# A two-layer mixer block on one core: the delta rule's gate rows built by other products, and a projection split around them

## The chip, the cores and the metric

The kernel runs on one core of a Trainium2 chip. The metric is the device time of one execution in microseconds (us); lower is better. Five engines work side by side, each on its own queue of instructions: TensorE (PE, matrix products, with PEld for its weight loads), VectorE (DVE), ScalarE (ACT), GpSimd (POOL) and SyncE (SP, which here issues the loads). They meet only by semaphores.

## The reference

A block of two equal layers works on 512 tokens of width 1024 in float32. Each layer normalises its input, projects it to four mixers (a gated delta rule, a dilated window attention, a stick-breaking attention and a retention), gates and adds their outputs, projects again, and ends with a feed-forward part. The change lies in the delta rule, of which this is the part that matters:

```python
beta = jax.nn.sigmoid(gdn_b.astype(f32)).transpose(0, 2, 1)
g = (-jnp.exp(a_log) * jax.nn.softplus(gdn_a + dt_bias)).transpose(0, 2, 1)
...
gc = jnp.cumsum(g.reshape(B, H, N, C), axis=-1)
decay = jnp.exp(jnp.where(incl, gc[..., :, None] - gc[..., None, :], -jnp.inf))
k_beta = k * beta[..., None]
lower = jnp.where(strict, jnp.einsum('bhncd,bhnsd->bhncs', k_beta, k) * decay, 0.0)
t_inv = triangular_solve(eye + lower, eye)
u = t_inv @ v_beta
w = t_inv @ (k_beta * jnp.exp(gc)[..., None])
...
state = state * jnp.exp(gl) + k_c.T @ v_new
```

There are four heads of width 128. The kernel takes chunks of 128 tokens, four of them, b = 0 to 3.

## The kernel before, in words

**Big products.** Every weight matrix streams in units of 256 rows. SP loads a unit into a stage, POOL splits it into a high and a low float32r part (L568 and L570), and `unit` (L1654, the products on L1686) multiplies: three products (high by high, low by high, high by low) for each of two row blocks and four column tiles, 24 products of 512 columns. The ring has four slots, and POOL may refill one when the first product of the next unit has run (`w_used`).

**PSUM.** Four banks `big0` to `big3` take projections. Four banks `mix0` to `mix3` take everything else. A list, `mixer_keys` (L274), names every use of a `mix` bank in order, and `number` (L215) deals them out in turn: use i of a layer goes to bank i mod 4, and must wait until the use before it in that bank is free. Before, a layer has 316 uses. The list starts again at `mix0` in the second layer, where `PER_LAYER` (L327) says how many uses of each bank the first had. The last four uses are the second feed-forward product of tokens 256 to 511 (`dn0` and `dn1` for t = 2 and 3; `dn0` is columns 0 to 511, `dn1` the rest), and the first uses of the next layer are the transposes of its normalised input for t = 2 and 3 (`turned`, L1734, key `pre1`).

**The delta rule.** Jobs `aq`, `ak`, `aab` and `av` project queries, keys, gate inputs and values. Between the units of `av` stand small jobs (`value_unit`, L1801): sums of squares after units 0 and 1, and after unit 2 the cumulative sum of the gates (key `gc`, L1810) and `decays(0)`. For chunk b and each head, `decays(b)` (L1826) makes in one bank the row of cumulative gates spread over all partitions (`R`: a gate column, broadcast, times the triangle of ones) and in another the row of betas (`B`: a beta column, broadcast, times the identity). These are eight float32 products of 128 columns, which the trace shows as 16 records.

ACT takes the exponential of `R` (L760). DVE waits for it, subtracts (L1301, L1302), clips (L1305) and multiplies the keys by `B` (L1310): `exponents`, L1297. Then ACT does its part (`pair_decays`, L762) and copies the four value tiles (`conv_raw`, L702, keys `raw` 8 to 11), and DVE convolves them (L1262 and L1264, four times three instructions). Behind those DVE has the chain of chunk 0: `lower` (L1316, L1318), `row_decays` (L1339, L1341, L1342), `first_level` (L1325, L1327), `scores_out` (L1332, L1334), and `exponents(1)`. PE runs a unit of a gate projection (`fill`), `lower(0)` and the scores, `decays(1)`, another unit, `lower(1)` and the scores (which need `exponents(1)`), another unit, and then the inversion levels. In the loop over chunks, `decays(2)` and `decays(3)` stand right before a `fill`.

**Waits that matter later.** `lower(b)` on PE waits for L1310 of the chunk. In the order of bank uses `R`, `B` of chunk 1 follow four places behind `raw` 10 and `raw` 11, so they wait until DVE has convolved those. A bank of the second feed-forward product is freed by `residual` (L1122, instruction L1127).

Of the kernel before, what the change touches and what calls it, by code (L numbers as in the profile page):

```python
# [17 lines left out]
F32R = mybir.dt.float32r  # L18
# [5 lines left out]
P = 128  # L24
# [41 lines left out]
def stick_at(e, j):  # L66
# [8 lines left out]

CI, CTU, CLV, CMG0, CMG1, CMG2, CSEL, CRD, CRR, CNTL, CNTU, CNEG, CEND = np.cumsum(
    [0, P, P, 7 * P, 512, P, P, 2 * DH, P, P, P, P, 8]).tolist()
ROT = CEND - CRD
# [7 lines left out]
def shape_constants():  # L86
# [16 lines left out]
    def rotation(half):  # L103
        r = np.zeros((P, P), np.float32)
        for b in range(0, P, DH):
            for i in range(half):
                r[b + i + half, b + i] = -1.0
                r[b + i, b + i + half] = 1.0
        return r
# [3 lines left out]
         neg(np.concatenate([first, near], 1)), neg(c <= p),  # L113
         neg((c <= p) & ((p - c) % 4 == 0)), sel, rotation(8), rotation(32), -one(c <= p), -one(c > p), -one(c + p >= 0)[:, 0:8]], 1)
    return np.ascontiguousarray(consts.astype(np.float32))
# [158 lines left out]
def mixer_keys():  # L274
# [3 lines left out]
    k += [("l2", i) for i in range(4)] + ["ab"] + [("l2", i) for i in range(4, 8)]  # L278
    k += ["gc", ("R", 0), ("B", 0)] + [("raw", i) for i in range(8, 12)]
    k += [("LT", 0), ("att", 0), ("R", 1), ("B", 1), ("LT", 1), ("att", 1)]  # L280
# [48 lines left out]
    "a_g": 2, "a_kbe": 4, "a_ln": 8, "a_lt": 4, "a_lt0": 4, "a_ltc": 4, "a_min": 4, "a_nrm": 4, "a_ohi": 4,  # L329
    "a_olo": 4, "a_out": 4, "a_qd": 4, "a_rs": 8, "a_sc": 3, "a_silu": 12, "a_small": 2, "a_smallact": 4, "a_sq": 8,  # L330
    "a_tap": 24, "a_z": 4, "an_rs": 4, "an_sq": 4, "b_exp": 36, "b_fc": 3, "b_fexp": 3, "b_max": 12, "b_nm": 12,
    "b_ohi": 5, "b_olo": 5, "b_rhi": 9, "b_rlo": 9, "b_rp": 9, "b_share": 2, "b_sum": 3, "b_zinv": 1, "b_zln": 1,
    "big_done0": 43, "big_done1": 43, "big_done2": 38, "big_done3": 38, "big_free0": 43, "big_free1": 43,
    "big_free2": 38, "big_free3": 38, "c_act": 40, "c_add": 8, "c_bias": 3, "c_exp": 20, "c_half": 4, "c_hi": 8,
    "c_ln": 20, "c_ohi": 4, "c_pos": 20, "c_pv": 4, "c_pvfree": 4, "c_split": 8, "c_sum": 20, "c_z": 20, "d_nrm": 4,
    "d_ohi": 4, "d_olo": 4, "d_out": 4, "d_rope": 4, "d_rp": 4, "dn_rs": 4, "dn_sq": 4, "f_hi": 32, "f_lo": 32,
    "f_relu": 32, "gated_b": 8, "gated_c": 8, "gated_d": 8, "m_hi": 8, "mix_done0": 79, "mix_done1": 79,
# [10 lines left out]
def hybrid_kernel(nc, ins, out):  # L348
    ctx = ExitStack()
    with ctx:  # L350
# [743 lines left out]
        def vector_layer(dve, l):  # L1094
# [133 lines left out]
            if l == 0:  # L1228
# [420 lines left out]
        def tensor_layer(pe, l):  # L1649
# [151 lines left out]
            def value_unit(i):  # L1801
                if i == 0:
                    l2_sums(0, 1, 2, 3)
                if i == 1:
                    gates_by_token()
                    l2_sums(4, 5, 6, 7)
                if i == 2:
                    pe.wait_ge(*upto("a_g", 2))
                    ps = tile_of("gc")
                    done(MM(ps[:, 0:16], triu, s_g.rearrange("p b h -> p (b h)"), start=True, stop=True), "gc")  # L1810
                    decays(0)

# [13 lines left out]
            def decays(b):  # L1826

                per_head_tile(("R", b), lambda o_, h: MM1(o_, s_g[:, b, h:h + 1].to_broadcast((P, P)), triu))
                per_head_tile(("B", b), lambda o_, h: MM1(o_, s_be[:, b, h:h + 1].to_broadcast((P, P)), ident))

# [12 lines left out]
            do("aab")  # L1843
            do("av", between=value_unit)
            set_fill("gatea0", "az")
# [474 lines left out]
```

## Time and profile before

| | |
|---|---|
| median of 3 runs | 2381.67 us (2379.85 to 2381.67) |
| the profiled execution | 2382.03 us, its span 2380.2 us |
| PE busy | 2340.7 us, 98% of the span |
| POOL / DVE / ACT busy | 1283.1 / 890.0 / 771.4 us |
| mean granted clock of PE | 0.996 |

The span is the part that the profiler covers. PE is the engine that hardly ever rests, and the chain that ended last is 91% PE. A record's length is longer than the distance to the next record, because products overlap: the distance between starts is what a product costs on a full PE. The two layers look alike: what stands at 92.51 us in the first stands at 1272.91 us in the second, 1180.4 us later, and so it goes for the rows around.

### The profile page before, as it was taken

Reading aid. Unit: us, or ns where it says so; the run is one execution under the profiler, and the core shown is the slowest. Engines: PE = TensorE matmul, PEld = TensorE weight load, DVE = VectorE, ACT = ScalarE, POOL = GpSimd, SP = SyncE. Lnnn points to the kernel's source line nnn. Section 1 sums busy time; section 2 is a strip of 40 time slices with the busy share of each in tenths; the row PEclk is TensorE's granted clock in tenths of the full one; section 3 lists DMA queues with packets and bytes.
Section 4 is the critical chain, followed back from the end, with each engine's and each line's share of the span. In section 5 each row is a group of like instructions: output and inputs, shape, how many; then the busy total and the mean of one; then the engine's idle time right before and its main releaser. Section 6 shows DMA issues by size and latency. Waiting matters only on the chain.

```text
span 2380.2 us, 29590 instructions
## 1 busy us (share of the span) xinstructions
PE 2340.7 (98%) x11798; PEld 1917.6 (81%) x11798; DVE 890.0 (37%) x1404; ACT 771.4 (32%) x1537; POOL 1283.1 (54%) x732
## 2 busy tenths in 40 slices
PE   8999999999999999999999999999999999999998
PEld 7798877787877888888887988767778778888887
DVE  3653314343355431123356523243443445211233
ACT  5533325323136231122355442262140353211121
POOL 5511653564553566677655126635555535666774
PEclk9999999999999999999999999999999999999999
DMA  4300331332231333333223013313322313333331
GB/s 152 98 27 28 89 89 53 98 89 72 79 100 44 106 107 97 98 98 98 80 77 89 19 36 91 87 47 113 89 80 71 93 49 95 119 98 97 97 95 66
DMA packets 105753, 196.84 MB, mean 83 GB/s; under 512 B 8464, under 2 KB 18832, under 8 KB 105360
## 3 DMA queue, kind: packets, MB, share of 16 engines
q1 hardware_dynamic: 104464, 188.65, 26.2%
q10 hardware_dynamic: 1152, 6.29, 0.8%
q8 instruction: 95, 1.56, 0.3%
q14 instruction: 42, 0.34, 0.0%
HBM read 192.82 MB, written 2.10 MB: 82 GB/s over the span
## 4 chain that ended last, share of the span: by engine, by line
PE 91%; DVE 5%; ACT 3%; issue 1%; DMA 0%; DVEq 0%; ACTq 0%
PE big L1686 66%; PE mix L1686 9%; PE mix L1824 5%; DVE c_lo L1429 1%; PE big L2000 1%; PE mix L1968 1%; PE mix L1894 1%; PE mix L2069 1%; PE mix L1979 1%; PE mix L1787 1%; PE mix L2201 1%; PE mix L2150 0%; DVE scr L1441 0%; PE mix L1741 0%; PE mix L2134 0%
## 5 line engine op out<-in xcount | busy, mean ns | idle before, releaser
L568 POOL TENSOR_SCALAR ring_hi<-stage 128x1024 fp32r<-128x1024 f32 (+3 forms) x364 | 372.1, 1022 | 1042.6 <-PE big L1686 962.2
L570 POOL TENSOR_TENSOR ring_lo<-stage,ring_hi 128x1024 fp32r<-128x1024 f32 (+3 forms) x364 | 912.6, 2507 | 30.4
L1686 PE MATMUL big<-h_hi,ring_hi 128*128 128x512 f32 (+1 forms) x1888 | 720.3, 382 | 2.8 <-DVE h_lo L1149 1.5
L1686 PE MATMUL big<-h_hi,ring_lo 128*128 128x512 f32 (+1 forms) x1888 | 709.9, 376 | 0.0
L1686 PE MATMUL big<-h_lo,ring_hi 128*128 128x512 f32 (+1 forms) x1888 | 709.9, 376 | 0.0
L1686 PEld LDWEIGHTS big<-h_hi,ring_hi 128*128 128x128 f32 x1888 | 355.7, 188 | 75.3 <-issue 9.0
L1686 PEld LDWEIGHTS big<-h_lo,ring_hi 128*128 128x128 f32 x1888 | 355.6, 188 | 65.4
L1686 PEld LDWEIGHTS big<-h_hi,ring_lo 128*128 128x128 f32 x1888 | 355.8, 188 | 63.8 <-issue 1.9
L1628 DVE TENSOR_TENSOR h_lo<-scr,h_hi 128x1024 fp32r<-128x1024 f32 x64 | 84.7, 1324 | 248.4 <-ACT h_hi L1067 248.4
L1686 PE MATMUL big<-ring_hi,h_hi 128*128 128x512 f32 x448 | 174.5, 391 | 0.0
L1686 PE MATMUL big<-ring_lo,h_hi 128*128 128x512 f32 x448 | 174.3, 391 | 0.0
L1686 PE MATMUL big<-ring_hi,h_lo 128*128 128x512 f32 x448 | 173.9, 390 | 0.0
L1067 ACT ACTIVATE h_hi<-scr 128x1024 fp32r<-128x1024 f32 x64 | 67.9, 1061 | 262.7 <-PE big L1686 260.7
L1639 DVE SCALAR_TENSOR_TENSOR scr<-big,scr 128x512 f32<-128x512 f32 x64 | 44.2, 691 | 254.5 <-ACT scr L1076 254.4
L1824 PE MATMUL mix<-scr 128*128 128x128 f32 (+1 forms) x1088 | 131.0, 276 | 1.3 <-DVE scr L1397 0.7
L1824 PEld LDWEIGHTS mix<-scr 128*128 128x128 f32 x1088 | 126.2, 192 | 4.6 <-DVE scr L1397 1.2
L1686 PE MATMUL mix<-ring_hi,h_hi 128*128 128x512 f32 x320 | 125.2, 391 | 0.0
L1686 PE MATMUL mix<-ring_hi,h_lo 128*128 128x512 f32 x320 | 124.7, 390 | 0.0
L1686 PE MATMUL mix<-ring_lo,h_hi 128*128 128x512 f32 x320 | 124.7, 390 | 0.0
L1076 ACT ACTIVATE scr<-big 128x512 f32<-128x512 f32 x64 | 38.3, 599 | 262.1 <-PE big L1686 261.2
L1686 PEld LDWEIGHTS big<-ring_hi,h_hi 128*128 128x128 f32 x448 | 84.1, 188 | 18.2 <-issue 0.7
L1686 PEld LDWEIGHTS big<-ring_hi,h_lo 128*128 128x128 f32 x448 | 84.2, 188 | 17.6
(292 smaller groups left out, 2826.3 us busy)
## 6 DMA issues: line engine op xcount, KB each, us to landing
stage<-in_w_in SPq DMA_DIRECT2D x168, 512.0 KB, 3.5
stage<-in_w_mlp_in SPq DMA_DIRECT2D x64, 512.0 KB, 3.6
stage<-in_w_mlp_out SPq DMA_DIRECT2D x64, 512.0 KB, 3.8
stage<-in_w_o SPq DMA_DIRECT2D x16, 512.0 KB, 3.8
stage<-in_w_br_a SPq DMA_DIRECT2D x8, 512.0 KB, 3.8
stage<-in_w_br_c SPq DMA_DIRECT2D x8, 512.0 KB, 3.8
stage<-in_w_br_d SPq DMA_DIRECT2D x8, 512.0 KB, 3.9
stage<-in_w_br_b SPq DMA_DIRECT2D x8, 512.0 KB, 3.5
```

Of the source, the lines that this page charges most:

```text
L568: nc.gpsimd.tensor_scalar(rH[jw][0:pp, r, 0:kk, 0:job.n], w, 1.0, 0.0, ALU.mult, ALU.add).then_inc(sem("w_hi"), 1)
L570: nc.gpsimd.tensor_tensor(rL[jw][0:pp, r, 0:kk, 0:job.n], w, f32(rH[jw][0:pp, r, 0:kk, 0:job.n]), ALU.subtract).then_inc(sem("w_ready"), 1)
L1067: A(hH[:, q:q + 2, :], fT[:, 2 * u:2 * u + 2, :], ACT.Copy).then_inc(sem("f_hi"), 1)
L1076: A(fT[:, 4 * g + i, :], ps[:, :], ACT.Relu).then_inc(sem("f_relu"), 1)
L1429: TT(c_L[:, us, :], c_S[:, us, :], f32(c_H[:, us, :]), ALU.subtract).then_inc(sem("c_split"), 1)
L1628: TT(hL[:, q:q + 2, :], fT[:, 2 * u:2 * u + 2, :], f32(hH[:, q:q + 2, :]), ALU.subtract).then_inc(sem("f_lo"), 1)
L1639: big_free(STT(fT[:, k, :], ps[:, :], 0.0, fT[:, k, :], ALU.max, ALU.mult), (f"up{g}", i))
L1686: ins_ = MM(o_, a_, r_, start=s0, stop=s1)
L1787: done(MM(ps[:, :], f32(ones_r[:, 0:1]).to_broadcast((P, P)), q_sq[:, i % 4, :], start=True, stop=True), ("l2", i))
L1824: return MM(o_, a_, b_, start=True, stop=True)
L1894: i = TR(ps[:, q * P:(q + 1) * P], g_T(e, h), ident)
L1968: i = MM(c_bank[u][:, at:at + w], hv(cK, h)[:, j * P:(j + 1) * P], hv(cQ, h)[:, j * P:], start=opens, stop=True, skip_group_check=True)
```

## The change

The gates and betas are no longer spread one head at a time. The cumulative gates and betas of all chunks (32 columns, `s_begc`) are transposed by two float32 products into a new `mix` use, key `gt`, in which even heads lie on partitions 0 to 15 and odd heads on 32 to 47. DVE splits them into a high float32r part and, 64 partitions further down, a low part, in a tile `g_rows` of 256 columns that was zeroed at the layer's start. `decays(b)` then is four float32r products of 256 columns (two for `R`, two for `B`): a new 16-column selector, broadcast, picks the four partitions of one row of the tile. `gc` moves one unit earlier, behind the sums of squares after unit 1. `decays(0)` moves from in front of `av`'s last unit into its middle, behind the column tiles 0 and 1. The list of bank uses becomes 317 long.

```diff
-    k += ["gc", ("R", 0), ("B", 0)] + [("raw", i) for i in range(8, 12)]
+    k += ["gc", "gt", ("R", 0), ("B", 0)] + [("raw", i) for i in range(8, 12)]
...
-    ... "mix_done0": 79, ... "mix_free0": 79, ...
+    ... "mix_done0": 80, ... "mix_free0": 80, ...
...
+        s_begc = st[:, 80:112].rearrange("p (r e) -> p e r", e=2)
...
+            V.memset(f32(g_rows[:, :]), 0.0).then_inc(sem("a_zero"), 1)
             V.memset(g_S, 0.0).then_inc(sem("a_S0"), 1)
...
+            ps = mix_wait(dve, "gt")
+            dve.wait_ge(*upto("a_zero", 1))
+            for e in range(2):
+                rows, cols = slice(32 * e, 32 * e + 16), slice(e * P, (e + 1) * P)
+                TS(g_rows[rows, cols], ps[rows, cols], 1.0, None, ALU.mult).then_inc(sem("a_rhi"), 1)
+            for e in range(2):
+                rows, low, cols = slice(32 * e, 32 * e + 16), slice(64 + 32 * e, 80 + 32 * e), slice(e * P, (e + 1) * P)
+                dve.wait_ge(*upto("a_rhi", e + 1))
+                i = TT(g_rows[low, cols], ps[rows, cols], f32(g_rows[rows, cols]), ALU.subtract)
+            mix_free(i, "gt")
...
                 if i == 1:
                     gates_by_token()
                     l2_sums(4, 5, 6, 7)
-                if i == 2:
                     pe.wait_ge(*upto("a_g", 2))
                     ps = tile_of("gc")
                     done(MM(ps[:, 0:16], triu, s_g.rearrange("p b h -> p (b h)"), start=True, stop=True), "gc")
-                    decays(0)
+                if i == 2:
+                    mix_freed(pe, "gc")
+                    ps = tile_of("gt")
+                    MM1(ps[0:16, 0:P], s_begc[:, 0, :], ident)
+                    done(MM1(ps[32:48, P:2 * P], s_begc[:, 1, :], ident), "gt")
...
             def decays(b):
 
-                per_head_tile(("R", b), lambda o_, h: MM1(o_, s_g[:, b, h:h + 1].to_broadcast((P, P)), triu))
-                per_head_tile(("B", b), lambda o_, h: MM1(o_, s_be[:, b, h:h + 1].to_broadcast((P, P)), ident))
+                mix_freed(pe, "gt")
+                for name, row in (("R", 8), ("B", 0)):
+                    ps = tile_of((name, b))
+                    for q in range(2):
+                        at = CROW - CRD + row + 2 * b + q
+                        i = MM1(ps[:, 2 * P * q:2 * P * (q + 1)], rot_r[:, at:at + 1].to_broadcast((P, P)), g_rows[:, :])
+                    done(i, (name, b))
...
-            do("av", between=value_unit)
+            for i in range(3):
+                unit(JOB["av"], i)
+                value_unit(i)
+            unit(JOB["av"], 3, (0, 1))
+            decays(0)
+            unit(JOB["av"], 3, (2, 3))
```

In the changed program every line number is higher: L1686 becomes L1699, L1741 becomes L1754, L1810 becomes L1822, L1824 becomes L1840.

First place, on PE, between the units 2 and 3 of `av` in the first layer, before:

```order
L1686 MATMUL big0<-h_lo,ring_hi 128x512
L1810 MATMUL mix1<-st,consts 128x16 [waits mix_free1,a_g]
L1824 MATMUL mix2<-consts,st 128x128 [waits mix_free2]
L1824 MATMUL mix2<-consts,st 128x128 x3
L1824 MATMUL mix3<-consts,st 128x128 [waits mix_free3]
L1824 MATMUL mix3<-consts,st 128x128 x3
L1686 MATMUL big1<-h_hi,ring_hi 128x512 [waits w_ready]
```

and now, where the rows left out are the rest of unit 3's first half (`big1` and `big2`):

```order
L1699 MATMUL big0<-h_lo,ring_hi 128x512
L1840 MATMUL mix2<-consts,st 16x128 [waits mix_free2,mix_free1]
L1840 MATMUL mix2<-consts,st 16x128
L1699 MATMUL big1<-h_hi,ring_hi 128x512 [waits w_ready]
...
L1699 MATMUL big2<-h_lo,ring_hi 128x512
L1840 MATMUL mix3<-g_rows_51,rot_r 128x256 [waits mix_free3,mix_free2]
L1840 MATMUL mix3<-g_rows_51,rot_r 128x256
L1840 MATMUL mix0<-g_rows_51,rot_r 128x256 [waits mix_free0]
L1840 MATMUL mix0<-g_rows_51,rot_r 128x256
L1699 MATMUL big3<-h_hi,ring_hi 128x512 [waits w_ready]
```

The first `R` (here in `mix3`) now comes behind twelve more products of 512 columns, and L1810 has left for the place one unit earlier.

Second place, on PE, after the first gate unit behind `av`: `lower(0)`, the scores and `decays(1)`, now:

```order
L1840 MATMUL mix1<-scr 128x128 [waits mix_free0,mix_free3,mix_free1,mix_free2]
L1840 MATMUL mix1<-scr 128x128 x3
L1840 MATMUL mix2<-scr 128x128 [waits mix_free2]
L1840 MATMUL mix2<-scr 128x128 x3
L1840 MATMUL mix3<-g_rows_51,rot_r 128x256 [waits mix_free3,mix_free2]
L1840 MATMUL mix3<-g_rows_51,rot_r 128x256
L1840 MATMUL mix0<-g_rows_51,rot_r 128x256 [waits mix_free0]
L1840 MATMUL mix0<-g_rows_51,rot_r 128x256
L1699 MATMUL big1<-h_hi,ring_hi 128x512 [waits w_ready]
```

Its order is that of before; the waits on `mix3` and `mix0` are for the convolutions of `raw` 10 and 11, as they were (then in `mix2` and `mix3`).

Third place, on PE, at the start of the second layer: the last product of `dn1` for t = 3 and the transposes for t = 2, before:

```order
L1686 MATMUL mix3<-ring_hi,h_hi 128x512 [waits w_ready]
...
L1686 MATMUL big1<-h_lo,ring_hi 128x256
L1741 MATMUL mix0<-consts,scr 128x128 [waits pre1_h,mix_free0]
L1741 MATMUL mix0<-consts,scr 128x128 x3
L1741 MATMUL mix1<-consts,scr 128x128 [waits pre1_h,mix_free1]
L1741 MATMUL mix1<-consts,scr 128x128 x3
L1686 MATMUL big2<-h_hi,ring_hi 128x256 [waits big_free2,w_ready]
```

and now:

```order
L1699 MATMUL mix0<-ring_hi,h_hi 128x512 [waits w_ready]
...
L1699 MATMUL big1<-h_lo,ring_hi 128x256
L1754 MATMUL mix0<-consts,scr 128x128 [waits pre1_h,mix_free0]
L1754 MATMUL mix0<-consts,scr 128x128 x3
L1754 MATMUL mix1<-consts,scr 128x128 [waits pre1_h,mix_free1]
L1754 MATMUL mix1<-consts,scr 128x128 x3
L1699 MATMUL big2<-h_hi,ring_hi 128x256 [waits big_free2,w_ready]
```

The transposes stand where they stood and go to the same bank, `mix0`; the bank's use before them is now `dn1` for t = 3, where it was `dn0` for t = 2.

## Rows read from the trace of the kernel before

**Rows 1.** The page: span and the chain that ended last, by engine.

```profile
span 2380.2 us, 29590 instructions
PE 91%; DVE 5%; ACT 3%; issue 1%; DMA 0%; DVEq 0%; ACTq 0%
```

**Rows 2.** Timeline of PE around `decays(0)`: start, length, engine, line, operation.

```profile
92.38 0.29 PE L1810 MATMUL mix<-st,consts 128*128 128x16 f32 x2
92.51 2.03 PE L1824 MATMUL mix<-consts,st 128*128 128x128 f32 x16
94.30 0.48 PE L1686 MATMUL big<-h_hi,ring_hi 128*128 128x512 f32 x1
94.61 0.40 PE L1686 MATMUL big<-h_hi,ring_lo 128*128 128x512 f32 x1
```

**Rows 3.** Timeline of PE, products of 256 columns in job `aq`.

```profile
26.61 0.28 PE L1686 MATMUL big<-h_hi,ring_lo 128*128 128x256 f32 x1
26.73 0.28 PE L1686 MATMUL big<-h_lo,ring_hi 128*128 128x256 f32 x1
```

**Rows 4.** Timeline of ACT, behind `decays(0)`.

```profile
93.69 0.60 ACT L760 ACTIVATE scr<-mix 128x512 f32<-128x512 f32 x1 [4.65 <-PE mix L1824]
96.30 0.63 ACT L764 ACTIVATE scr<-scr 128x512 f32<-128x512 f32 x1 [2.01 <-DVE scr L1305]
```

**Rows 5.** Timeline of DVE from `exponents(0)` to the chain of chunk 1.

```profile
95.21 1.05 DVE L1305 TENSOR_SCALAR scr<-scr 128x512 f32<-128x512 f32 x1
...
98.15 1.53 DVE L1262 SCALAR_TENSOR_TENSOR scr<-mix,lw,scr 128x511 f32<-128x511 f32 x2 [1.29 <-ACT scr L709]
...
106.39 0.75 DVE L1264 SCALAR_TENSOR_TENSOR scr<-mix,lw,scr 128x509 f32<-128x509 f32 x1
...
108.39 0.16 DVE L1339 COPY st<-scr 128x4 f32<-128x4 f32 x1
...
109.74 0.70 DVE L1325 TENSOR_TENSOR mix<-mix,consts 128x512 f32<-128x512 f32 x1
...
113.20 0.43 DVE L1305 TENSOR_SCALAR scr<-scr 128x512 f32<-128x512 f32 x1
...
116.81 0.98 DVE L1339 COPY st<-scr 128x4 f32<-128x4 f32 x1
...
118.31 2.88 DVE L1342 TENSOR_TENSOR scr<-scr 128x512 f32<-128x512 f32 x1
121.11 0.69 DVE L1325 TENSOR_TENSOR mix<-mix,consts 128x512 f32<-128x512 f32 x1
```

**Rows 6.** Timeline of POOL in the same stretch.

```profile
94.94 1.05 POOL L568 TENSOR_SCALAR ring_hi<-stage 128x1024 fp32r<-128x1024 f32 x1 [3.96 <-PE big L1686]
...
116.72 1.05 POOL L568 TENSOR_SCALAR ring_hi<-stage 128x1024 fp32r<-128x1024 f32 x1 [3.58 <-PE big L1686]
117.86 2.77 POOL L570 TENSOR_TENSOR ring_lo<-stage,ring_hi 128x1024 fp32r<-128x1024 f32 x1
```

**Rows 7.** Timeline of PE: `decays(1)`, the unit behind it, `lower(1)`.

```profile
107.10 1.95 PE L1824 MATMUL mix<-consts,st 128*128 128x128 f32 x16
108.81 0.47 PE L1686 MATMUL big<-h_hi,ring_hi 128*128 128x512 f32 x1
...
114.36 1.97 PE L1824 MATMUL mix<-scr 128*128 128x128 f32 x16
```

**Rows 8.** Timeline of PE, the unit behind `decays(3)`.

```profile
168.41 0.48 PE L1686 MATMUL big<-h_hi,ring_hi 128*128 128x512 f32 x1
```

**Rows 9.** Timeline of DVE beside it.

```profile
167.85 0.16 DVE L1339 COPY st<-scr 128x4 f32<-128x4 f32 x1
```

**Rows 10.** Timeline of PE, transposes for t = 2 of the second layer.

```profile
1197.54 1.24 PE L1741 MATMUL mix<-consts,scr 128*128 128x128 f32 x8
```

**Rows 11.** Timeline of DVE, the two residuals of t = 3.

```profile
1200.10 1.41 DVE L1127 SCALAR_TENSOR_TENSOR x_sb<-mix,st,x_sb 128x512 f32<-128x512 f32 x2
```

**Rows 12.** Busy time by stretch: PE, PEld, DVE, ACT, POOL, PE clock, DMA, GB/s.

```profile
16.00:19.00 3.00, 2.89 (x13) 2.92 (x14) 1.46 (x8) 2.16 (x8) 2.94 (x2) 0.50 1.06 389
```

More of the change, by code:

```diff
@@ L73 @@
 RING = 4
-CI, CTU, CLV, CMG0, CMG1, CMG2, CSEL, CRD, CRR, CNTL, CNTU, CNEG, CEND = np.cumsum(
-    [0, P, P, 7 * P, 512, P, P, 2 * DH, P, P, P, P, 8]).tolist()
+CI, CTU, CLV, CMG0, CMG1, CMG2, CSEL, CRD, CRR, CNTL, CNTU, CNEG, CROW, CEND = np.cumsum(
+    [0, P, P, 7 * P, 512, P, P, 2 * DH, P, P, P, P, 8, 16]).tolist()
 ROT = CEND - CRD
@@ L113, in shape_constants @@
          neg(np.concatenate([first, near], 1)), neg(c <= p),
-         neg((c <= p) & ((p - c) % 4 == 0)), sel, rotation(8), rotation(32), -one(c <= p), -one(c > p), -one(c + p >= 0)[:, 0:8]], 1)
+         neg((c <= p) & ((p - c) % 4 == 0)), sel, rotation(8), rotation(32), -one(c <= p), -one(c > p), -one(c + p >= 0)[:, 0:8], one(p % 32 == c)[:, 0:16]], 1)
     return np.ascontiguousarray(consts.astype(np.float32))
@@ L329 @@
     "a_g": 2, "a_kbe": 4, "a_ln": 8, "a_lt": 4, "a_lt0": 4, "a_ltc": 4, "a_min": 4, "a_nrm": 4, "a_ohi": 4,
[L330 to L337, printed above, removed]
[1 row of a table removed]
+    "a_olo": 4, "a_out": 4, "a_qd": 4, "a_rhi": 2, "a_rs": 8, "a_sc": 3, "a_silu": 12, "a_small": 2, "a_smallact": 4,
+    "a_sq": 8, "a_tap": 24, "a_z": 4, "a_zero": 1, "an_rs": 4, "an_sq": 4, "b_exp": 36, "b_fc": 3, "b_fexp": 3,
+    "b_max": 12, "b_nm": 12, "b_ohi": 5, "b_olo": 5, "b_rhi": 9, "b_rlo": 9, "b_rp": 9, "b_share": 2, "b_sum": 3,
+    "b_zinv": 1, "b_zln": 1, "big_done0": 43, "big_done1": 43, "big_done2": 38, "big_done3": 38, "big_free0": 43,
+    "big_free1": 43, "big_free2": 38, "big_free3": 38, "c_act": 40, "c_add": 8, "c_bias": 3, "c_exp": 20, "c_half": 4,
+    "c_hi": 8, "c_ln": 20, "c_ohi": 4, "c_pos": 20, "c_pv": 4, "c_pvfree": 4, "c_split": 8, "c_sum": 20, "c_z": 20,
+    "d_nrm": 4, "d_ohi": 4, "d_olo": 4, "d_out": 4, "d_rope": 4, "d_rp": 4, "dn_rs": 4, "dn_sq": 4, "f_hi": 32,
+    "f_lo": 32, "f_relu": 32, "gated_b": 8, "gated_c": 8, "gated_d": 8, "m_hi": 8, "mix_done0": 80, "mix_done1": 79,
[1 row of a table added]
     "mixed_b": 8, "n2_half": 4, "n2_ln": 4, "n2_nw": 8, "n2_ss": 8, "n2_v": 4, "n2_w": 8, "n2_y": 4, "n4_half": 4,
@@ L367, in hybrid_kernel @@
         idb, strictb = (nc.alloc_sbuf_tensor_at(n, [P, P], BF16, offset=scr_at + 4 * at) for n, at in (("idb", 19456), ("strictb", 19520)))
+        g_rows = nc.alloc_sbuf_tensor_at("g_rows", [P, 2 * P], F32R, offset=scr_at + 4 * 19712)
         c_hi = nc.alloc_sbuf_tensor_at("c_hi", [P, 5 * S], F32R, offset=scr_at + 4 * C_HIGH)
```

2 rows, old and new, of the table PER_LAYER are left out of this document.

## The prediction, made before the changed kernel was run

> **What bounds the kernel now.** I read the page first: a span of 2380.2 us whose last chain is 91% PE [rows 1]. So each us taken from PE is worth a us, unless something else is late in its place. The change is local, so I then went through the timelines of PE, DVE, ACT and POOL from 90 to 185 us, and looked for the moments in which PE stands against another engine. There are two kinds. DVE works without a break from its first value convolution at 98.15 to the end of `exponents(1)`; PE's `lower(1)` at 114.36 starts just when that is done [rows 5, 7]. And at the start of layer 2 the transposes for t = 2 begin at 1197.54, while DVE's last residual ends at 1200.10 + 1.41 = 1201.51 [rows 10, 11]. Nothing waits for that residual there now. Both layers show the same rows 1180.4 us apart, so all below but the layer border counts twice.
>
> **The products themselves.** Sixteen records of `decays(1)` take 108.81 - 107.10 = 1.71 us, 0.107 each; `decays(0)` takes 94.30 - 92.51 = 1.79 [rows 2, 7]. A float32r product of 256 columns costs 26.73 - 26.61 = 0.12 [rows 3], with another stationary matrix each time, so four cost 0.48. Going from float32 to float32r lengthens one gap (0.31 between 94.30 and 94.61, where 0.23 is usual), once before and once after. `decays` of chunks 1 to 3 thus lose 1.23 each, `decays(0)` 1.31. The two transposes of `gt` are four records more, 0.43. `gc` only moves; it takes 0.13 either way. If nothing else were late, a layer would win 3 x 1.23 + 1.31 - 0.43 = 4.57, the kernel 9.1.
>
> **Layer part, step 1: `R` of chunk 0 comes later.** `gt` ends at 92.51 + 0.43 = 92.94. Twelve products of unit 3 at 0.227 (24 of them and a switch took 114.36 - 108.81 = 5.55, [rows 7]) and one switch of 0.08 bring PE to 95.74. The second `R` product starts at 95.86. Before, ACT began L760 at 93.69, 0.40 after the last `R` record had started (92.51 + 7 x 0.11) [rows 2, 4]; so now 96.26, which is 2.57 later. DVE's clipping L1305 started at 95.21 and took 1.05 because POOL's L568 ran from 94.94; alone it takes 0.43 [rows 5, 6]. Now it starts at 97.78, POOL has finished both its instructions by then, and it ends at 98.21 where it was 96.26: ACT's L764 starts 1.95 later than at 96.30 [rows 4]. The value copies and convolutions follow in the same queues: DVE starts them at 100.10 instead of 98.15 and ends them at 109.09 instead of 107.14 [rows 5].
>
> DVE's four new instructions (two copies of 16 rows, two subtractions) have to fit between 93.2 and 95.74. The nearest rows are a small copy at 0.16 alone and at 0.98 when POOL is in the way [rows 5]. Four times 0.16 is hidden; four times 0.98 would cost 1.4 more. I take nothing: the value is nearer to the free copy, since a copy out of PSUM is not the kind that the rows show stretched, and even one stretched instruction is hidden. The memset at the layer's start is hidden too (0.16 to 1.05, with all of `aq`, `ak` and most of `av` between it and its reader). The earlier `gc` needs gates that DVE has had since before; no wait is added.
>
> **Step 2: PE waits at `decays(1)`.** PE ends `av` at 95.74 + 0.48 + 2.72 = 98.94, the gate unit at 104.38, `lower(0)` and scores (16 records like `decays` and a switch, 1.78) at 106.16. `R` waits for the third convolution, `B` for the fourth: 109.14. The next unit starts at 109.4, where it was 108.81 [rows 7]. So all that PE won so far is gone, and 0.6 us more. Behind the waiting `B` stand the unit and `lower(1)`.
>
> **Step 3: the unit's start sends POOL into DVE's chain.** POOL's L568 starts 0.64 after the first product of a unit (94.94 - 94.30) [rows 2, 6]: at 110.04. DVE's L1339 comes 1.25 after the last convolution (108.39 - 107.14), at 110.34. That is the meeting that chunk 1 already shows: L568 at 116.72, L1339 at 116.81 stretched to 0.98, L570 at 117.86, and L1342 stretched to 2.88 (L1325, of the same size, takes 0.69), so that L1325 starts at 121.11, 4.39 after L568 [rows 5, 6]. In chunk 0 it was missed, and L1325 started at 109.74. Now it starts at 110.04 + 4.39 = 114.43, which is 4.69 later. Only 1.95 of it is step 1; 2.74 is the collision. `exponents(1)` ends 4.69 later, and PE, which is ready at 109.4 + 5.44 = 114.84, starts `lower(1)` at 114.36 + 4.69 = 119.05. From there to the inversion all engines keep the distances they had. Step 3 lies between 0 (no meeting) and 2.74; by the row nearest in kind, chunk 1's, I take 2.74.
>
> The Trainium skill ("SBUF — State Buffer", section "Who interferes with whom") says that a DVE instruction with two SBUF inputs, or in its two-port mode, and a GpSimd instruction never share their ports: the second one blocks. The trace agrees, with the 2.88. By that rule the collision is all or nothing, so a middle value would be wrong.
>
> **Step 4: `decays(2)`** keeps its 1.23: PE's next needs of DVE there are several us old, and what follows waits for PE's own `lower(2)`.
>
> **Step 5: `decays(3)`.** Its unit starts at 168.41 [rows 8], and relative to DVE it would start 1.23 earlier, at 167.18; POOL follows at 167.82, DVE's L1339 stands at 167.85 [rows 9]. So here too the unit would come just early enough to put L568 and L570 in front of L1342, which ACT's L760 waits for. Between 1.23 kept and 0.1 lost; I take 0.3 kept, since the rows have POOL first, if only by 0.03.
>
> Per layer: + 4.69 - 1.23 - 0.3 = + 3.2, so + 6.4 for two.
>
> **The border of the layers.** 317 uses are one more than four times 79. The transposes for t = 2 now wait for `dn1` of t = 3, which is freed at 1201.51, and start at 1201.56 instead of 1197.54: + 4.0, once. Nothing hides it: PE is in order, and behind it stand the whole of `aq`'s first half. What ACT and DVE do for t = 3 slides along by 2.5 to 4 us and stays ahead of PE. There is no deadlock, since the residual needs nothing of these transposes. The bound below is 0, if that bank were free sooner than the row says; above, the 4.0.
>
> **Sum.** 6.4 + 4.0 = 10.4 us on top of the profiled 2382.03 us. Counted from the median of 2381.67, which is 0.4 lower and what the time will be compared with, that is **2392.1 us**.
>
> **The rivals.**
> *The clock falls in the new pauses.* After the sparse start PE ran at the lower level: from 16 to 19 us the granted clock was 0.50 (1.2 GHz), after PE had waited for its first inputs [rows 12]. That stretch cost half of 2.89, 1.4 us. The new pauses of about 4 us (twice before `lower(1)`, once at the border) have no like in the trace of before. For it speaks their length, against it that PE is full on both sides. One to three times 1.4: 2393.5 to 2396.3. The Trainium skill ("TensorE: Matmul & The Clock Gate", section "HAM oscillation") says that idle gaps put the array back to half rate. By it this rival is real; no row here shows it behind a full PE.
>
> *No collision.* If POOL misses DVE in both places, a layer changes by 1.95 - 1.23 - 1.23 = - 0.5, two by - 1.0, and the border remains: 2384.7. For it speaks that 0.3 us decides in step 3; against it that both sides hang on the same event, the last convolution.
>
> *The border costs nothing*, steps 1 to 5 as told: 2381.67 + 6.4 = 2388.1. For it speaks only that the bank numbers are read from a list and not from a row.
>
> *The other side: faster.* If `decays(0)` in the middle of unit 3 delays nobody, because ACT and DVE catch up in the 1.29 us that DVE idles before 98.15 and behind it, PE keeps its 9.1 us. With the border that is 2381.67 - 9.1 + 4.0 = 2376.6, without it 2372.6. It decides in its favour if `lower(1)` starts before about 112.2. Against it: those 1.29 us are ACT's own chain behind L1305, which moves as a whole, and from there DVE has no gap.
>
> **How the numbers follow.** Chances: the forecast 0.48, the falling clock 0.18, the border for nothing 0.10, no collision 0.13, faster 0.11. From no change this measurement can tell about 0.2%, 4.8 us. Forecast, clock and free border lie above 2386.4: slower 0.76. No collision is + 3.0: same 0.13. Faster 0.11. The range goes from the no-collision case, 2384.3, to the clock's upper end, 2396.5, and leaves out the faster case and a little above.
>
> **What would show it.** Right: PE's first `R` product at about 95.7; the first value convolution near 100.1; a pause of PE of about 2 us before `B` of chunk 1 and of about 4 us before `lower(1)`, with L1342 of chunk 0 stretched to over 2 us; the transposes of layer 2 about 4 us behind the last half-width product before them; PE's busy time less by 7 to 10 us although the span is longer. Wrong: no stretched L1342 in chunk 0 (step 3), the convolutions less than 1 us later (step 1), a `decays` that takes over 1 us (the products), or a granted clock of 0.5 anywhere after 20 us (the first rival).

## The result, and the profile after

The changed kernel takes 2393.96 us (median of 5 runs, 2393.00 to 2394.73), the kernel before 2381.67 (5 runs, 2379.85 to 2382.12): a ratio of 1.0056, 95% interval 1.0046 to 1.0067. It is slower by 12.3 us by the medians (13.3 by the ratio); 2392.1 was forecast.

The page of the changed kernel, against [rows 1], with the waits of PE summed over the execution (line waited at, releaser, us in total, times, longest):

```profile
span 2392.2 us, 29436 instructions
PE 2336.6 (98%) x11710; PEld 1911.8 (80%) x11710; DVE 896.1 (37%) x1414; ACT 771.8 (32%) x1537; POOL 1284.8 (54%) x732
PE 88%; DVE 6%; ACT 3%; issue 2%; DMA 0%; DVEq 0%; ACTq 0%
```

```profile
PE mix L1840 <- DVE scr L1323: 9.4, 4, 3.8
...
PE mix L1754 <- DVE x_sb L1129: 4.1, 1, 4.1
...
PE mix L1840 <- DVE scr L1267: 2.4, 2, 1.2
...
PE big L1699 <- ACT scr L711: 1.9, 2, 1.0
```

PE has less to do (2336.6 us against 2340.7), the span is 12 us longer, and the last chain has 3% less of PE. The four waits are new, and each names a place: L1840 is `decays` and `lower`, L1754 the transposes at the layer border, L1699 a weight unit. Line numbers are 2 to 26 higher than before: L1305 is now L1318, L1310 L1323, L1339 L1352, L1342 L1355, L1325 L1338, L568 L570.

PE in the first layer, answering to [rows 2, 7]: start, length, engine, line, operation, count, and in brackets how long it stood and for whom.

```profile
95.26 0.64 PE L1840 MATMUL mix<-g_rows,rot_r 128*128 128x256 f32 x4
95.74 0.40 PE L1699 MATMUL big<-h_hi,ring_hi 128*128 128x512 f32 x1
...
99.61 0.47 PE L1699 MATMUL big<-h_hi,ring_hi 128*128 128x512 f32 x1 [0.95 <-ACT scr L711]
...
106.89 0.48 PE L1840 MATMUL mix<-g_rows,rot_r 128*128 128x256 f32 x2
108.55 0.50 PE L1840 MATMUL mix<-g_rows,rot_r 128*128 128x256 f32 x2 [1.18 <-DVE scr L1267]
```

```profile
118.34 2.66 PE L1840 MATMUL mix<-scr 128*128 128x128 f32 x16 [3.83 <-DVE scr L1323]
```

The four products of `decays(0)` take 95.74 - 95.26 = 0.48 us where sixteen took 1.79. And then PE stands: 1.18 before `B` of chunk 1, 3.83 before `lower(1)`. What it stands for is in DVE's timeline, answering to [rows 5], and POOL's, answering to [rows 6]:

```profile
99.50 1.53 DVE L1265 SCALAR_TENSOR_TENSOR scr<-mix,lw,scr 128x511 f32<-128x511 f32 x2 [1.28 <-ACT scr L711]
...
109.74 0.78 DVE L1352 COPY st<-scr 128x4 f32<-128x4 f32 x1
110.42 0.68 DVE L1354 TENSOR_TENSOR scr<-scr 128x512 f32<-128x512 f32 x1
111.03 2.88 DVE L1355 TENSOR_TENSOR scr<-scr 128x512 f32<-128x512 f32 x1
113.83 0.68 DVE L1338 TENSOR_TENSOR mix<-mix,consts 128x512 f32<-128x512 f32 x1
...
121.79 1.53 DVE L1355 TENSOR_TENSOR scr<-scr 128x512 f32<-128x512 f32 x1
```

```profile
109.44 1.05 POOL L570 TENSOR_SCALAR ring_hi<-stage 128x1024 fp32r<-128x1024 f32 x1 [5.66 <-PE big L1699]
110.58 2.77 POOL L572 TENSOR_TENSOR ring_lo<-stage,ring_hi 128x1024 fp32r<-128x1024 f32 x1
```

The first value convolution starts at 99.50 instead of 98.15, on a trace whose start happened to be 0.6 us shorter (the sums of `l2` start at 82.75 instead of 83.35), so 1.95 later. PE begins the next unit behind `B`, POOL's split of the weights starts 0.55 us after that, and DVE's L1355, which takes 0.68 alone, takes 2.88 beside POOL's L572.

The border, answering to [rows 10, 11], and the granted clock behind the two long pauses (window; length, busy PE, PEld, DVE, ACT, POOL; the third number from the end is the clock):

```profile
1204.73 1.71 PE L1754 MATMUL mix<-consts,scr 128*128 128x128 f32 x8 [4.13 <-DVE x_sb L1129]
```

```profile
114.00:118.00 4.00, 0.51 (x3) 0.09 (x1) 3.90 (x8) 0.86 (x2) 0.00 (x0) 1.00 0.48 133
118.00:119.00 1.00, 0.66 (x5) 0.66 (x6) 0.29 (x1) 0.45 (x2) 0.00 (x0) 1.00 0.00 0
119.00:120.00 1.00, 1.00 (x10) 1.00 (x9) 0.46 (x1) 0.00 (x0) 0.00 (x0) 0.81 0.00 0
120.00:122.00 2.00, 2.00 (x8) 1.80 (x8) 1.82 (x5) 0.60 (x1) 0.40 (x1) 0.50 0.00 0
122.00:123.00 1.00, 1.00 (x4) 0.72 (x3) 1.00 (x1) 0.00 (x0) 0.92 (x2) 0.50 0.00 0
123.00:124.00 1.00, 1.00 (x6) 0.82 (x5) 0.96 (x3) 0.00 (x0) 1.00 (x1) 0.99 0.00 0
...
1206.00:1208.00 2.00, 2.00 (x12) 2.00 (x11) 1.13 (x4) 2.00 (x8) 1.92 (x2) 0.50 0.59 135
```

PE stands from about 114.5 to 118.3, goes on at the full clock (1.00), and a microsecond later is at 0.50, the lower of its two levels, until about 123. The same follows the wait at the border.

**Where the 12 us are.** The starts of like records in both traces, after minus before: -0.60 at the sums of `l2`, +3.98 at `lower(1)`, +4.69 at the end of chunk 1's inversion (129.08 against 124.39), +3.41 behind `decays(2)`, +3.18 ahead of the border, +8.37 behind it, then +12.74 at `lower(1)` of layer 2 and +11.96 in the end. So the first layer costs 3.8 (3.18 and the 0.60), the second 3.6 and the border 5.2.

### The profile page after: what moved, and what is told of

Same layout as the page of the kernel before. It is cut to its first block, busy times and chain, and to the rows that moved or that the text cites. A ratio compares the mean times of both kernels' runs of the same rounds, so it can differ in the third digit from the quotient of the medians.

```text
span 2392.2 us, 29436 instructions
## 1 busy us (share of the span) xinstructions
PE 2336.6 (98%) x11710; PEld 1911.8 (80%) x11710; DVE 896.1 (37%) x1414; ACT 771.8 (32%) x1537; POOL 1284.8 (54%) x732
## 4 chain that ended last, share of the span: by engine, by line
PE 88%; DVE 6%; ACT 3%; issue 2%; DMA 0%; DVEq 0%; ACTq 0%
PE big L1699 65%; PE mix L1699 9%; PE mix L1840 5%; DVE c_lo L1442 1%; PE big L2026 1%; PE mix L1994 1%; PE mix L1920 1%; PE mix L2095 1%; PE mix L2005 1%; PE mix L1800 1%; DVE scr L1355 1%; DVE scr L1265 1%; PE mix L2227 0%; PE mix L2176 0%; DVE scr L1454 0%
## 5 line engine op out<-in xcount | busy, mean ns | idle before, releaser
L570 POOL TENSOR_SCALAR ring_hi<-stage 128x1024 fp32r<-128x1024 f32 (+3 forms) x364 | 371.4, 1020 | 1052.8 <-PE big L1699 972.2
L572 POOL TENSOR_TENSOR ring_lo<-stage,ring_hi 128x1024 fp32r<-128x1024 f32 (+3 forms) x364 | 914.9, 2514 | 30.4
L1699 PE MATMUL big<-h_hi,ring_hi 128*128 128x512 f32 (+1 forms) x1888 | 720.1, 381 | 4.6 <-ACT scr L711 1.9
L1699 PE MATMUL big<-h_hi,ring_lo 128*128 128x512 f32 (+1 forms) x1888 | 710.5, 376 | 0.0
L1699 PE MATMUL big<-h_lo,ring_hi 128*128 128x512 f32 (+1 forms) x1888 | 710.3, 376 | 0.0
L1699 PEld LDWEIGHTS big<-h_hi,ring_hi 128*128 128x128 f32 x1888 | 356.5, 189 | 77.0 <-issue 11.4
L1699 PEld LDWEIGHTS big<-h_lo,ring_hi 128*128 128x128 f32 x1888 | 356.3, 189 | 65.9
L1699 PEld LDWEIGHTS big<-h_hi,ring_lo 128*128 128x128 f32 x1888 | 356.6, 189 | 63.3 <-issue 1.4
L1699 PE MATMUL big<-ring_lo,h_hi 128*128 128x512 f32 x448 | 174.3, 391 | 0.0
L1699 PE MATMUL big<-ring_hi,h_hi 128*128 128x512 f32 x448 | 174.3, 391 | 0.0
L1699 PE MATMUL big<-ring_hi,h_lo 128*128 128x512 f32 x448 | 173.9, 390 | 0.0
L1840 PE MATMUL mix<-scr 128*128 128x128 f32 (+1 forms) x1088 | 134.1, 280 | 10.8 <-DVE scr L1323 9.4
L1840 PEld LDWEIGHTS mix<-scr 128*128 128x128 f32 x1088 | 128.3, 195 | 15.7 <-DVE scr L1323 10.6
L1699 PE MATMUL mix<-ring_hi,h_hi 128*128 128x512 f32 x320 | 125.1, 391 | 0.0
L1699 PE MATMUL mix<-ring_hi,h_lo 128*128 128x512 f32 x320 | 124.7, 390 | 0.0
L1699 PE MATMUL mix<-ring_lo,h_hi 128*128 128x512 f32 x320 | 124.7, 390 | 0.0
L1699 PEld LDWEIGHTS big<-ring_hi,h_hi 128*128 128x128 f32 x448 | 84.2, 188 | 18.1 <-issue 0.7
L1699 PEld LDWEIGHTS big<-ring_lo,h_hi 128*128 128x128 f32 x448 | 83.8, 188 | 18.2 <-POOL ring_lo L572 1.1
```

Of the source, the lines that this page charges most:

```text
L570: nc.gpsimd.tensor_scalar(rH[jw][0:pp, r, 0:kk, 0:job.n], w, 1.0, 0.0, ALU.mult, ALU.add).then_inc(sem("w_hi"), 1)
L572: nc.gpsimd.tensor_tensor(rL[jw][0:pp, r, 0:kk, 0:job.n], w, f32(rH[jw][0:pp, r, 0:kk, 0:job.n]), ALU.subtract).then_inc(sem("w_ready"), 1)
L1699: ins_ = MM(o_, a_, r_, start=s0, stop=s1)
L1840: return MM(o_, a_, b_, start=True, stop=True)
```

## The experiments

All were timed beside the kernel before, whose medians in the three sessions were 2379.94 (e1 to e4), 2380.26 (e5 to e8) and 2379.93 us (e9 to e11). Ratios are to it. The changed kernel was timed in a session of its own, where the kernel before took 2381.67; so a distance to it is given twice, by the medians and by the ratios. The interval of a ratio is some 2 to 3 us to either side, so smaller differences between experiments rest on the traces. In kernels with the gate (e2) or ACT's order (e6) the line numbers are up to 4 higher again.

**e1: the border alone mended**, by another order of the last four bank uses:

```diff
-    k += [(f"dn{hf}", t) for t in (2, 3) for hf in range(2)]
+    k += [("dn1", 2), ("dn0", 3), ("dn1", 3), ("dn0", 2)]
```

> The changed kernel with the four last bank uses of a layer dealt in another order, so that the first transposes of layer 2 again go to a bank that dn0 of t = 2 used before. Theory (the border of the layers costs a wait and, behind it, a stretch at the lower clock): PE starts those transposes without the 4.1 us wait and keeps the full clock there, 4.1 + 1.1 = 5.2 us less than the changed kernel's 2393.96, so about 2388.8 us, ratio to the kernel before 1.0030. Rival A (the clock falls there anyway): 2389.9. Rival B (the bank is not what the transposes wait for): no change, 2394.

Measured: 2388.40 us, ratio 1.0036 (1.0024 to 1.0049), 5.6 us under the changed kernel by the medians, 4.8 by the ratios. The wait for `x_sb` is gone and the clock is 1.00 from 1190 to 1215; it still falls behind the pause at 118. By the times the border cost 4.8 to 5.6, with some 3 us of interval, and 5.2 in the trace; 4.0 was forecast.

**e4: the border alone put into the kernel before**, by an order that gives the transposes the same late bank:

```diff
-    k += [(f"dn{hf}", t) for t in (2, 3) for hf in range(2)]
+    k += [("dn1", 3), ("dn1", 2), ("dn0", 3), ("dn0", 2)]
```

> The kernel before, with nothing changed but the order of the four last bank uses, so that the first transposes of layer 2 go to the bank that dn1 of t = 3 used. Theory: the border's wait appears here alone, 4.0 us, and with it the lower clock for about 2.2 us of products: 2381.67 + 5.1 = 2386.8 us, ratio 1.0021. Rival A (the clock falls only together with what else the change does): 2385.7. Rival B (another part of the change makes the border wait): 2381.7.

Measured: 2385.66, ratio 1.0026 (1.0016 to 1.0035): 5.7 us slower by the medians and 6.2 by the ratio, with nothing else changed. The theory's difference was 5.1, that of rival A 4.0; the time alone doesn't part the two, but the trace does. The wait is there with the same length, and the clock falls with it:

```profile
PE mix L1741 <- DVE x_sb L1127: 4.1, 1, 4.1
```

```profile
1202.00:1204.00 2.00, 1.72 (x9) 1.72 (x9) 0.23 (x1) 0.57 (x3) 2.00 (x2) 0.50 0.47 176
1204.00:1206.00 2.00, 2.00 (x12) 2.00 (x11) 1.30 (x5) 2.00 (x9) 1.92 (x2) 0.50 0.79 214
```

So the border is 4.1 of wait and some 1 to 2 of clock, from both sides.

**e2: POOL held back.** Its split waits until DVE has done the L1355 of that chunk:

```diff
+                chained = {3: 1, 4: 2, 6: 3}.get(u - UNIT_AT["gatea0", 1])
+                if chained:
+                    pool.wait_ge(*upto("a_kbe", chained))
```

> The changed kernel with GpSimd held back: before it splits the three weight units that fall next to DVE's row_decays (chunks 0, 1 and 3), it waits until DVE has finished them. Theory (POOL's two instructions block DVE's two-input instructions, and that is most of what lower(1) waits for): L1355 of chunk 0 takes 0.69 instead of 2.88 us, lower(1) comes only about 2 us later than before instead of 4.6, the clock doesn't fall behind it, decays(3) keeps its 1.2 us. About 5 us less per layer, 10 in all: 2384 us, ratio to before 1.001. Rival (DVE's chain is late for the later R alone): L1355 is short but lower(1) still comes over 4 us late, and the time stays within 2 us of 2394. Second rival (holding POOL back starves PE of weights): slower than 2394, with PE waiting for POOL's L574.

Measured: 2385.69, ratio 1.0023 (1.0013 to 1.0033), 8.3 us under the changed kernel (7.9 by the ratios); 10 was expected. PE and DVE of e2:

```profile
116.15 2.05 PE L1843 MATMUL mix<-scr 128*128 128x128 f32 x16 [1.26 <-DVE scr L1326]
```

```profile
110.13 0.16 DVE L1355 COPY st<-scr 128x4 f32<-128x4 f32 x1
110.20 0.68 DVE L1357 TENSOR_TENSOR scr<-scr 128x512 f32<-128x512 f32 x1
110.80 0.68 DVE L1358 TENSOR_TENSOR scr<-scr 128x512 f32<-128x512 f32 x1
```

The small copy is back from 0.78 to 0.16 and the 2.88 to 0.68; the pause before `lower(1)` shrinks from 3.83 to 1.26, and the clock is 1.00 from 110 to 125. The inversion of chunk 1 ends 4.2 us earlier counted from the sums of `l2`; twice that is 8.4. No wait of PE for POOL came in its place, so the second rival is out.

**e8: the gate for chunk 0 alone** (`{3: 1}`).

> The changed kernel with POOL held back for chunk 0 alone; chunks 1 and 3 collide as they did. My step 3: this collision costs 2.74 a layer, 2.2 by the row of lower(1), and the pause falls under the length behind which the clock fell, 0.7 more: -5.8 in two layers, 2388.2, ratio 1.0035. Rival: all that the gate won (8.3 us) comes from chunk 0, the others collide for nothing: 2385.7, ratio 1.0023. Other rival: the clock falls behind a pause of 1.3 to 2 us as well: 2389.5.

Measured: 2388.38, ratio 1.0032 (1.0020 to 1.0045), 5.6 under the changed kernel (5.7 by the ratios): the theory's number, 2388.2, though the interval also holds the two rivals. The collision of chunk 0 costs 2.8 us a layer with the clock that fell behind it. The other chunks collide for 1.1 to 1.3 more, by the difference to e2; the times alone would not show that, but the trace does: L1358 of chunk 1 is 2.88 again, and PE stands 0.33 and 0.24 in the inversion and 0.85 in chunk 3, where e2 has 0, 0 and 0.15.

**e3: border and gate.**

> Both edits together. Theory: the two costs are separate in time and add, 2394 - 5.2 - 10 = 2378.8 us, ratio 0.9988. Rival (they share something, such as the clock): less than the sum, over 2381.

Measured: 2379.10, where 2378.8 was expected; ratio 0.9995 (0.9986 to 1.0003). Within the intervals the two costs add up: 4.8 and 7.9 by the ratios make 12.7, and both mends together bring 14.5. Without them the kernel can't be told from the one before, though PE has less to do. What is left is step 1, which neither mend touches: `lower(1)` still comes 2.0 later than before, counted from the sums of `l2` (32.99 against 31.01).

**e10: the place alone.** The kernel before, its float32 `decays` untouched, no `gt`, no change at the border:

```diff
-            do("av", between=value_unit)
...
+            unit(JOB["av"], 3, (0, 1))
+            decays(0)
+            unit(JOB["av"], 3, (2, 3))
```

> The kernel before with its float32 decays as they were, no g_rows and no gt, only the place of the change: decays(0) between the halves of unit 3. The count of bank uses and the border stay as before. Theory: the place is what costs, by DVE's chain: R of chunk 0 is 12 products at 0.227 and a switch, 2.8 us, later, L1305 loses its 0.6 of being stretched, DVE's convolutions start 2.2 later, PE waits at decays(1), and its unit then sends POOL into L1342 of chunk 0, 2.7 more. 4 to 5 us a layer: 2389.5, ratio 1.004. Rival: without the fourfold faster products PE comes to decays(1) later and waits little, so POOL misses L1342: 2 us a layer or less, under 2385. Second rival: place costs nothing (under 2382) and the products' own chain through DVE is to blame.

Measured: 2387.23, ratio 1.0027 (1.0017 to 1.0038): slower by 7.3 by the medians and 6.4 by the ratio, less than the theory's 9.6 and more than the 5.1 that its rival allowed. The interval (4 to 9 us) doesn't quite exclude that rival, and three of the eight runs, the profiled one among them, lie at 2383.9 to 2384.8, the others at 2387.0 to 2388.0. In the trace the end of chunk 1's inversion comes 2.9 later than before, counted from the sums of `l2` (43.91 against 41.04). PE stands 0.53 before `B` of chunk 1 and 1.19 before `lower(1)`. DVE and POOL of e10:

```profile
99.86 1.53 DVE L1262 SCALAR_TENSOR_TENSOR scr<-mix,lw,scr 128x511 f32<-128x511 f32 x2 [1.28 <-ACT scr L709]
...
110.77 1.53 DVE L1342 TENSOR_TENSOR scr<-scr 128x512 f32<-128x512 f32 x1
```

```profile
110.46 1.30 POOL L568 TENSOR_SCALAR ring_hi<-stage 128x1024 fp32r<-128x1024 f32 x1 [6.31 <-PE big L1686]
111.84 2.72 POOL L570 TENSOR_TENSOR ring_lo<-stage,ring_hi 128x1024 fp32r<-128x1024 f32 x1
```

The convolutions are 2.1 later (99.86 - 98.15, and 0.39 of a shorter start), as expected. L1342 met POOL's first instruction instead of its second, so it was stretched to 1.53 and not to 2.88. So the half-way place is a loss in itself, also without new products: some 3 us a layer. The second rival is out.

**e5: `decays(0)` one tile earlier**, on top of e3:

```diff
-            unit(JOB["av"], 3, (0, 1))
+            unit(JOB["av"], 3, (0,))
             decays(0)
-            unit(JOB["av"], 3, (2, 3))
+            unit(JOB["av"], 3, (1, 2, 3))
```

> The changed kernel with the border's banks in the old order, POOL's splits held back behind L1342 of the chunk, and decays(0) one tile earlier in unit 3 (after the first of its four tiles). Theory: the products are worth their 1.23 us each wherever PE is what the end hangs on, and what the change lost was the place of decays(0) and the two collisions of its consequences. One tile of unit 3 is three hi/lo products plus a weight switch less ahead of R, some 1.4 us, so the first convolution starts 0.5 us after the kernel before's instead of 1.95, PE waits at decays(1) for about 0 and a layer wins 1.23 (decays(2)) + 1.23 (decays(3)) + some of decays(1): 2375 us, ratio 0.998 of the kernel before. Rival: ACT's order (L760 behind what has been queued since) decides, not PE, and the tile earlier is worth nothing: 2379, ratio 0.9995, as with the two mends alone.

Measured: 2377.71, ratio 0.9987 (0.9979 to 0.9996). Between theory (2375) and rival (2379). `R` came 1.36 earlier, but DVE's clipping then met POOL again and took 1.01 instead of 0.43, so the convolutions came only some 0.75 earlier.

**e11: `decays(0)` before the whole of unit 3**, on top of e3, straight behind `gt`.

> The changed kernel with border and gate mended, and decays(0) before the whole of unit 3, straight behind gt, as the kernel before had it. PE then stands about 1.3 us for DVE's four instructions that make g_rows (in e5 the first tile of unit 3, 1.36 us, lay over them). Theory: PE waits 1.2 us before decays(1) anyway, so this stand only takes the place of that wait and DVE's chain starts as in e5: the same as e5 within 1 us, 2378.0, ratio 0.999. Rival: PE's stand adds to the end, 1.3 a layer: 2380.3, ratio 1.0000.

Measured: 2376.02, ratio 0.9982 (0.9973 to 0.9991). The theory expected e5 within 1 us; this is 1.7 under it by the medians and 1.2 by the ratios. PE of e11:

```profile
93.94 0.73 PE L1843 MATMUL mix<-g_rows,rot_r 128*128 128x256 f32 x4 [1.37 <-DVE g_rows L1310]
...
107.12 0.72 PE L1843 MATMUL mix<-g_rows,rot_r 128*128 128x256 f32 x4
```

PE stands 1.37 us in the open, and the kernel is not slower for it: the wait inside `decays(1)` is gone in exchange. Filling that gap with half a unit, as the change did (e3), cost 3.1 us more by the ratios, whose intervals just overlap.

**e6: e5, and ACT makes the first raw copy before the pair exponentials of chunk 0:**

```diff
             key_decays(0)
+            conv_raw(8)
             pair_decays(0)
-            for i in range(8, 12):
+            for i in range(9, 12):
                 conv_raw(i)
```

> The same, and ACT makes the first raw copy of av before the exponentials of chunk 0's pair, so that DVE has a convolution to do in the 1.28 us that it stood idle. Theory: DVE's unbroken row from the first value convolution to exponents(1) is what PE's lower(1) hangs on, so an earlier first convolution is worth up to 1 us a layer: 2373 us, ratio 0.997. Rival: ACT's other instructions slide behind by the same 0.6 us and the L764 that DVE's own chunk 0 needs comes late: nothing, 2375.

Measured: 2372.34, where 2373 was expected; ratio 0.9969 (0.9956 to 0.9981). This beats both kernels: by the ratio it is 7.4 us under the one before. PE of e6:

```profile
107.20 0.50 PE L1844 MATMUL mix<-g_rows,rot_r 128*128 128x256 f32 x2 [0.29 <-DVE scr L1271]
114.40 2.05 PE L1844 MATMUL mix<-scr 128*128 128x128 f32 x16 [1.25 <-DVE scr L1327]
```

Counted from the sums of `l2`, `lower(1)` comes 1.4 us earlier than in e5, against the 1 that was expected. The rival's 2375 is still inside the interval, but by it this start would not have moved.

**e9: the same order of ACT in the kernel before**, with the gate for its chunk 1. **e7: that gate alone** (`{4: 2}`).

> The kernel before, with the two mends that do not need the change: ACT makes the first raw copy of av before the pair exponentials of chunk 0, and POOL's split of chunk 1 waits behind L1342. Theory: before the change PE is without a gap up to lower(1), so an earlier DVE has nothing to give; what e6 won, it won because the shorter decays left PE room. 2379.5 us, ratio 0.9997 of the kernel before. Rival: ACT's order is the gain in itself and the products only came with it: ratio 0.998 or less, under 2376.

> The kernel before, with nothing changed but POOL's split of the ring behind L1342 of chunk 1, whose 2.88 us the trace of before shows. Theory of the collision (a blocked DVE instruction costs what it is longer than 0.69, as far as PE waits on it): PE waited 1.4 for L1327 in chunk 1, so 0.6 us a layer: 2378.7 against 2379.9, ratio 0.9995, hardly to be told from none; L1342 then takes about 0.7 in the trace. Rival: POOL's split, 3.8 us later, makes the next unit late: PE waits on the ring, and the time is over 2381.

Measured: e9 2382.02, ratio 1.0003 (0.9995 to 1.0012); e7 2380.01, ratio 1.0001 (0.9992 to 1.0010). ACT's order is worth nothing there: `lower(1)` starts 31.0 us behind the sums of `l2` in e7, in e9 and in the kernel before, as PE is without a gap. So what e6 won needs the shorter `decays`. For e7 1.2 us less was expected, too little to be told from none. Its trace has chunk 1's inversion end 1.0 us earlier in layer 1, and the times don't show the 2 us that this would make in two layers (see the last section).

## Why the prediction was right

*The products* were right: 0.48 us for `decays(0)` and 170.57 - 170.02 = 0.55 for `decays(3)`, where 0.48 was said. PE's busy time fell by only 4.1 us where 7 to 10 was named as a sign; the records at the slower clock are longer, by some 4.5 us in all (an estimate from the trace: 1.7 a layer and 1.1 at the border, see below), and 4.1 + 4.5 = 8.6.

*Step 1* was right to the digit: convolutions 1.95 later. It missed a wait: the first tile of the gate unit needs the bank of the first `av` tile, which ACT frees only after its own delayed chain (0.95 at 99.61). It cost nothing, since PE had to stand before `B` anyway: the pause there was 1.18 and not the 2 that was said, as the other 0.95 had been stood before.

*Step 2* was right. The unit after `decays(1)` starts at 108.89 + 0.60 = 109.49; 109.4 was said.

*Step 3* was right, and e2 and e8 show its cause: `lower(1)` moved by 3.98 + 0.60 = 4.58 where 4.69 was forecast. But the sentence drawn from the page "SBUF — State Buffer" of the Trainium skill (section "Who interferes with whom"), that a middle value would be wrong, is not borne out. How much is lost depends on which of POOL's two instructions it meets: the 0.68 us instruction took 1.53 beside the first (which took 1.19 in chunk 1 of the changed kernel and 1.30 in e10) and 2.88 beside the second, of 2.77 us.

*Step 4* was right: +5.29 at the end of chunk 1's inversion and +4.01 behind `decays(2)`, both with the 0.60 added, so 1.28 was kept where 1.23 was said.

*Step 5*: `decays(3)` kept 0.23, 0.3 was said. The collision in chunk 3 is there as forecast:

```profile
171.25 0.95 DVE L1352 COPY st<-scr 128x4 f32<-128x4 f32 x1
...
172.71 2.88 DVE L1355 TENSOR_TENSOR scr<-scr 128x512 f32<-128x512 f32 x1
```

*The border*: the wait is 4.13, 4.0 was said.

*The range* was given as 2384.3 to 2396.5, where the cases that it names come to 2384.7 and 2396.3; the measured time lies within either.

*What failed* is the rival that was set beside the forecast instead of in it: the clock. It fell behind all three pauses of about 4 us. At the border it cost 1.1 in the trace (5.2 less 4.1). In a layer it cost 1.7. Here are the starts of the inversion of chunk 1 and of what follows it, first before and then now:

```profile
121.62 0.60 PE L1860 MATMUL mix<-consts,scr 128*128 128x128 f32 x4
...
124.39 3.69 PE L1824 MATMUL mix<-scr 128*128 128x128 f32 x32
```

```profile
127.34 1.03 PE L1886 MATMUL mix<-consts,scr 128*128 128x128 f32 x8
...
129.08 3.69 PE L1840 MATMUL mix<-scr 128*128 128x128 f32 x32
```

From the start of `lower(1)` to the end of the unit behind it PE takes 127.34 - 118.34 = 9.00 us, where it took 121.62 - 114.36 = 7.26. The inversion itself takes 1.74 where it took 2.77, as PE stands for DVE no more in it, so only 0.7 is added to the end. That is 2.5 us in all with two layers and the border, the shorter start gives 0.6 back, and 10.4 + 2.5 - 0.6 = 12.3. The medians are 12.3 apart and the traces 12.0; that the sum meets the medians to the digit is chance. So the clock is the term of the sum that was put at nothing, and the forecast of 2392.1 is 1.9 too low for it.

I gave the clock 0.18 since no row showed it falling behind a full PE. There were such rows, later in the same trace. The kernel before, at the same place of both layers:

```profile
760.55 6.77 PE L2201 MATMUL mix<-scr,consts 3*128 3x512 f32 x14
```

```profile
764.00:770.00 6.00, 6.00 (x11) 2.88 (x11) 5.04 (x8) 3.23 (x5) 1.70 (x2) 0.50 0.00 0
...
1942.00:1951.00 9.00, 9.00 (x22) 4.50 (x22) 7.04 (x10) 5.50 (x7) 2.80 (x2) 0.63 0.00 0
```

From 755 to 760 PE is full, at 1.00. Then come 14 products of three rows in 6.8 us, and the clock is 0.50 from 764 to 770. So a clock of 0.50 "anywhere after 20 us", which was named as a sign of being wrong, stood in the kernel before already and could tell nothing. With these rows the falling clock would have had a place in the sum, though they show it behind thin products and not behind a pause, and so not its size. With the sizes measured since, 1.1 and twice 0.7, the sum is 2394.6.

*The faster rival* supposed that `decays(0)` in the middle of unit 3 delays nobody. Step 1 and e10 show that it does; e11 and e6 show what there was to gain without that delay.

## What to carry to other kernels

When an engine that bounds a kernel gets faster at one place, look at what its neighbours start because of it: here PE came to a weight unit earlier relative to DVE, and POOL's split, started by that unit, landed on a DVE instruction in the critical chain. Work moved ahead to fill a gap of the busy engine also delays whoever waits for what comes behind it: an open gap of 1.4 us was cheaper than the half unit put into it. And one more use in a ring of four banks changes the partner of every later use, so a change counts the ring's uses up to the end of the loop, not only where it edits.

## What the runs showed that was not expected

A pause of 3.8 to 4.1 us on a full PE went with a fall of the granted clock to 0.50 in each trace that has one (changed kernel, e1, e2, e4, e8); none followed pauses of 1.2 to 1.4 us (e2, e3, e6, e11). The length varies: in layer 1 of the changed kernel the fall comes a microsecond after PE has gone on and is over at 123; in e2's border the clock is 0.50 from 1200 to 1206, right from the first product on, in e4's until 1208.

The times of one kernel can lie in two groups: e7 has six from 2378.03 to 2380.01 and five from 2382.75 to 2383.07. The traces differ most in one place, the thin stretch near 1945 us (the 14 products of three rows). The mean clock from 1920 to 1970 us is 0.97 in the profiled runs of e3, e7 and e10, all of the lower group of their kernels, 0.93 in the kernels before and after, and 0.90 in e9, whose profiled run is of the upper group. The 14 thin products there take 4.9 to 5.0 us in e3, e7 and e10, 6.3 and 6.5 in the kernels before and after, and 7.1 in e9. Not all runs fit: e11's profiled run is of its lower group and has 0.93, and e5's, whose times form one group, has 0.90. Here e3 and e9:

```profile
1920.00:1970.00 50.00, 49.66 (x224) 35.92 (x225) 27.08 (x39) 20.51 (x28) 23.57 (x16) 0.97 0.23 69
```

```profile
1920.00:1970.00 50.00, 49.16 (x220) 34.14 (x219) 23.78 (x36) 22.61 (x31) 19.24 (x13) 0.90 0.21 66
```

From 0.97 to 0.90 is 0.07 x 50 = 3.5 us of full-speed work lost (an estimate), near the distance of the groups. How long PE stays at the lower level behind a thin stretch thus seems to vary between runs; that this makes the two groups, and that it hides the 2 us of e7, was not shown and stays open.
